# A DeltaNet stage with its steps turned: first blocks substituted on VectorE, level products on small tiles, seven weight halves subtracted on GpSimd

## The reference

```
qkv = silu(causal_conv(proj[..., :GD_QKV], conv_w))      # 4 taps
G = cumsum(g) within a chunk
gamma = exp(where(incl, G[..., :, None] - G[..., None, :], -inf))
a_mat = where(strict, kk * gamma * beta, 0)
t_mat = triangular_solve(a_mat + eye, eye)               # inverse of a unit lower triangle
u = t_mat @ (v * beta);  w = t_mat @ (k * beta * exp(G))
step: v_new = u - w S;  o = q_g S + qk v_new;  S = decay S + k_g^T v_new
out = (rmsnorm(o) * gain * silu(z)) @ w_out
```

## Time and profile before

| | us |
|---|---|
| median of 3 runs | 2547.61 (2543.11 to 2550.33) |
| the profiled execution | 2547.9 |
| its span | 2545.8 |
| TensorE busy | 2377.2 (93%) |
| VectorE busy | 1282.2 (50%) |
| ScalarE busy | 960.3 (38%) |
| GpSimd busy | 486.9 (19%) |
| chain that ended last: TensorE's share | 83% |
| transfers: mean rate | 80 GB/s |

### The profile page before, as it was taken

How to read it: one execution, slowest core, us unless ns; L and a number is a source line. 1 busy time by engine, 2 the same in 40 slices (tenths; PEclk the granted TensorE clock), 3 DMA queues, 4 the chain that set the end, 5 groups by cost and what they waited for, 6 DMA issues and landing times.

```text
span 2545.8 us, 30868 instructions
## 1 busy us (share of the span) xinstructions
PE 2377.2 (93%) x10878; PEld 1942.2 (76%) x10878; DVE 1282.2 (50%) x1548; ACT 960.3 (38%) x1313; POOL 486.9 (19%) x384
## 2 busy tenths in 40 slices
PE   8999998998999999999999975989898889999997
PEld 7888876787788888788888754777777667888886
DVE  5544337665364443554443685455555442644533
ACT  5233335554443233333233454333333343423332
POOL 2222001100221110111111235343121101211100
PEclk9999999998999999999999996899899999999999
DMA  5332332221223323233333220111111213223232
GB/s 166 95 94 77 101 107 63 69 72 66 66 84 98 99 82 96 86 99 99 99 82 94 73 85 10 40 50 51 50 50 52 73 50 98 72 94 99 85 97 66
DMA packets 67561, 203.11 MB, mean 80 GB/s; under 512 B 8320, under 2 KB 12544, under 8 KB 67488
## 3 DMA queue, kind: packets, MB, share of 16 engines
q1 hardware_dynamic: 67488, 202.13, 25.5%
HBM read 199.94 MB, written 2.16 MB: 79 GB/s over the span
## 4 chain that ended last, share of the span: by engine, by line
PE 83%; DVE 6%; ACT 4%; issue 4%; POOL 2%; DMA 0%; DVEq 0%; SPq 0%; ACTq 0%; POOLq 0%
PE bank L1413 70%; PE bank L1595 6%; ACT w_hi L503 1%; DVE gate L1048 1%; POOL gd_o L1348 1%; POOL sq L1345 1%; PE bank L1680 1%; DVE up L1048 1%; DVE pre L1042 1%; PE bank L1693 1%; PE bank L1722 1%; PE bank L1560 0%; DVE w_lo L845 0%; PE bank L1714 0%; PE bank L1686 0%
## 5 line engine op out<-in xcount | busy, mean ns | idle before, releaser
L845 DVE TENSOR_TENSOR w_lo<-raw,w_hi 128x1024 fp32r<-128x1024 f32 x405 | 586.2, 1465 | 563.1 <-ACT w_hi L503 563.0
L1413 PE MATMUL bank<-h_hi,w_hi 128*128 128x512 f32 x1760 | 702.8, 399 | 44.3 <-DVE h_lo L849 31.3
L1413 PE MATMUL bank<-h_hi,w_lo 128*128 128x512 f32 x1760 | 692.4, 393 | 0.0
L1413 PE MATMUL bank<-h_lo,w_hi 128*128 128x512 f32 x1696 | 666.4, 393 | 0.0
L503 ACT ACTIVATE w_hi<-raw 128x1024 fp32r<-128x1024 f32 x405 | 426.4, 1055 | 538.1 <-PE bank L1413 533.3
L1413 PEld LDWEIGHTS bank<-h_hi,w_hi 128*128 128x128 f32 x1760 | 335.3, 191 | 123.5 <-issue 40.3
L1413 PEld LDWEIGHTS bank<-h_hi,w_lo 128*128 128x128 f32 x1760 | 334.6, 190 | 71.5
L1413 PEld LDWEIGHTS bank<-h_lo,w_hi 128*128 128x128 f32 x1696 | 323.0, 190 | 69.5 <-issue 3.1
L1287 POOL TENSOR_TENSOR y<-y,up 128x512 f32<-128x512 f32 x88 | 173.9, 1976 | 744.6 <-DVE up L888 671.2
L1413 PE MATMUL bank<-act_hi,w_hi 128*128 128x512 f32 x704 | 277.4, 394 | 0.0
L1413 PE MATMUL bank<-act_hi,w_lo 128*128 128x512 f32 x704 | 276.0, 392 | 0.0
(11 more groups left out here) (254 smaller groups left out, 2467.6 us busy)
## 6 DMA issues: line engine op xcount, KB each, us to landing
raw<-in_ffn_in SPq DMA_DIRECT2D x172, 512.0 KB, 3.5
raw<-in_gd_in SPq DMA_DIRECT2D x49, 512.0 KB, 5.5
raw<-in_ffn_out SPq DMA_DIRECT2D x64, 384.0 KB, 3.1
raw<-in_ffn_out SPq DMA_DIRECT2D x64, 320.0 KB, 2.9
raw<-in_hg_in SPq DMA_DIRECT2D x32, 512.0 KB, 3.5
raw<-in_gd_out SPq DMA_DIRECT2D x16, 512.0 KB, 3.7
raw<-in_hg_out SPq DMA_DIRECT2D x8, 512.0 KB, 3.4
g_bc<-g_rows SPq DMA_DIRECT2D x8, 512.0 KB, 4.3
```

What stands on the lines that cost most here:

```text
L845: nc.vector.tensor_tensor(w_lo[:, r, :], raw[:, r, :], w_hi[:, r, :].bitcast(f32), ALU.subtract).then_inc(lo_split, 1)
L1413: ins = nc.tensor.matmul(dst, w, moving[ml][:, k, :], start=first and n == 0 and (wl, ml) == (0, 0), stop=last and n == len(ks) - 1 and wl ...
```

## The change

**Turned steps.** `step(j)` now runs the recurrence of group j - 1 first and then the levels of group j; group 0's levels come before step 1, and `last_step` has only the recurrence of group 7. TensorE's step is written with named pieces; `each` is 2 in step 1 and 1 else. Step 1 has seven units (10 to 16), steps 2 to 7 five, the last two. Units 5 to 7 change places (query first). The sums and products of keys 4 to 7 move into step 1.

```diff
+                    new_values(g, 0)
+                    piece(each)
+                    state_add(g, 0)
+                    piece(each)
+                    attend(g, 0)
+                    for t in (1, 2):
+                        state_read(g, t)
+                        piece(each)
+                        new_values(g, t)
+                        piece(each)
+                        state_add(g, t)
+                        piece(each)
+                        attend(g, t)
+                    state_read(g, 3)
+                    piece(each)
+                    new_values(g, 3)
+                    if level:
+                        key_gram(j)
+                        key_transpose(j)
+                    piece(each)
+                    attend(g, 3)
+                    piece(2 * each)
+                    out_sums(g)
+                    if level:
+                        piece(4)
...
+                            late_key_sum(5)
+                        piece()
+                        level_p5(j)
+                        piece(2)
...
+                        level_t5(j)
+                        scores(j)
+                        piece()
+                        value_transpose(j, 0)
+                        piece(2)
+                        level_u5(j)
+                        piece(2)
...
+                            late_key_product(5)
+                        piece(2)
+                        level_p6(j)
+                        piece(2)
```

```diff
+                def to_lanes_first():
+                    dve.wait_ge(kkd_made, 4)
+                    for b in range(4):
+                        rows = slice(b * SUB, (b + 1) * SUB)
+                        src = four_banks[rows, :].rearrange("p (n q) -> p q n", q=P)[:, rows, :]
+                        nc.vector.transpose(lane_t[rows, :, :], src.unsqueeze(2).to_broadcast([SUB, SUB, 2, 4 * NT])).then_inc(lane_kk, 1)
+                    lanes_done(0)
+
+                def to_lanes_second():
+                    dve.wait_ge(kkd_copied, 4)
+                    dve.wait_ge(diag_ready, 2)
+                    nc.vector.transpose(lane_t, kk_diag.unsqueeze(2).to_broadcast([P, SUB, 2, 4 * NT])).then_inc(lane_kk, 1)
+                    lanes_done(1)
+
+                def substitute(cols):
+
+                    for c in cols:
+                        rows = SUB - 1 - c
+                        part = lane_tmp[:, 0:rows * c].rearrange("p (i k) -> p i k", k=c)
+                        below = lane_t[:, c + 1:SUB, 0:c]
+                        if c == 1:
+                            dve.wait_ge(lane_ready, 2)
+                        wait(dve, lane_sub, 2 * (c - 1))
+                        TT(part, lane_t[:, c + 1:SUB, c:c + 1].to_broadcast([P, rows, c]),
+                           lane_t[:, c:c + 1, 0:c].to_broadcast([P, rows, c]), ALU.mult).then_inc(lane_sub, 1)
+                        dve.wait_ge(lane_sub, 2 * (c - 1) + 1)
+                        TT(below, below, part, ALU.add).then_inc(lane_sub, 1)
 
```

```diff
+                def lo(n):
+                    u = first_unit[s] + n
+                    pool.wait_ge(lo_split, u + SKEW)
+                    pool.wait_ge(hi_split, u + 1 + SKEW)
+                    TTp(w_lo[:, u % RING, :], raw[:, u % RING, :], w_hi[:, u % RING, :].bitcast(f32), ALU.subtract).then_inc(lo_split, 1)
+                lo(6)
+                lo(7)
                 pool.wait_ge(lanes_loaded, 16 * 8)
                 TTp(lane_w[:], lane_g[:, 0, :, :], lane_g[:, 1, :, :], ALU.subtract).then_inc(lane_w_ready, 1)
```

```diff
+                def level_p5(n):
+                    pe.wait_ge(at_ready, 2 * (n + 1))
+                    pe.wait_ge(base_ready, n + 1)
+                    pe.wait_ge(q_logged, 1)
+                    for n_t in range(TILES):
+                        cols = slice(n_t * SUB, (n_t + 1) * SUB)
+                        MM(bank[3][32:64, cols], at[0:32, n_t, 32:64], half_6[0:32, n_t, 0:SUB], start=True, stop=True)
+                        ins = MM(bank[3][96:128, cols], at[64:96, n_t, 96:128], half_6[64:96, n_t, 0:SUB], start=True, stop=True)
+                    ins.then_inc(p5_made, 1)
+
+                def level_t5(n):
+                    pe.wait_ge(p5_ready, n + 1)
+                    pe.wait_ge(kt_ready, n + 1)
+                    for n_t in range(TILES):
+                        ins = MM(bank[4][32:64, n_t * SUB:(n_t + 1) * SUB], inv_t[32:64, n_t, 32:64], prod5[32:64, n_t, :], start=True, stop=True)
+                    ins.then_inc(t5_made, 1)
+
+                def level_u5(n):
+                    pe.wait_ge(vt_ready, 2 * n + 1)
+                    for n_t in range(TILES):
+                        cols = slice(n_t * SUB, (n_t + 1) * SUB)
+                        MM(bank[5][0:32, cols], prod5[32:64, n_t, :], inv_t[32:64, n_t, 32:64], start=True, stop=True)
+                        ins = MM(bank[5][64:96, cols], prod5[96:128, n_t, :], inv_t[96:128, n_t, 96:128], start=True, stop=True)
+                    ins.then_inc(u5_made, 1)
+
+                def level_p6(n):
+                    pe.wait_ge(t5_ready, n + 1)
+                    if n:
+                        pe.wait_ge(vt_ready, 2 * n + 2)
+                    for n_t in range(TILES):
+                        ins = MM(bank[6 if n else 2][CH:P, n_t * CH:(n_t + 1) * CH], at[0:CH, n_t, CH:P], half_6[0:CH, n_t, :], start=True, stop=True)
+                    ins.then_inc(p6_made, 1)
+
+                def level_u6(n):
+                    pe.wait_ge(p6_ready, n + 1)
+                    pe.wait_ge(u5_ready, n + 1)
+                    for n_t in range(TILES):
+                        ins = MM(bank[3][0:CH, n_t * CH:(n_t + 1) * CH], half_6[CH:P, n_t, :], inv_t[CH:P, n_t, CH:P], start=True, stop=True)
+                    ins.then_inc(u6_made, 1)
+
+                def new_values(g, t):
```

**VectorE's step**, for g > 0 (the taps stand in brackets):

```diff
+                    else:
                         gate_out(g - 1, 1)
+                        memory(g, 0)
+                        if j == 4:
...
+                        residual(g, 1)
+                        if j == 2:
+                            to_lanes_second()
+                        out_gate(g - 1, 1)
+                        value_decay(g, 1)
+                        memory(g, 1)
+                        residual(g, 2)
+                        value_decay(g, 2)
+                        query_drain(j)
+                        memory(g, 2)
+                        query(j, (0,))
+                    residual(g, 3)
+                    query(j, (1,))
+                    lo(n0 + 4)
+                    query(j, (2, 3))
+                    log_gamma(j, 0)
+                    log_gamma(j, 1)
+                    value_drain(j, 0)
+                    value(j, 0, (0, 1, 2))
+                    out_norm(g)
+                    decayed_keys(j)
+                    if g == 0:
+                        key_norm(4)
+                        key_norm(5)
...
+                    value(j, 0, (3,))
+                    lo(n0 + 5)
+                    query_norm(j)
+                    value_drain(j, 1)
+                    value(j, 1, (0,))
+                    lo(n0 + 6)
+                    probs_out(j)
+                    if g == 0:
+                        key_norm(6)
+                        key_norm(7)
+                    value(j, 1, (1, 2, 3))
+                    gate_out(g, 0)
+                    lo(n0 + 7)
+                    out_gate(g, 0)
```

More of the change, by code:

```diff
@@ L708, in out_root, with out_square @@
+                def out_square(g):
+                    for e in range(2):
+                        act.wait_ge(og_made, 2 * g + e + 1)
+                        wait(act, og_ready, 2 * (g - 1) + e + 1)
+                        nc.scalar.activation(y[:, e, :], bank[(7, 2)[e]][:], ACT.Square).then_inc(og_squared, 1)
                 def out_root(g):
@@ new lines, in log_gamma, with decayed_keys @@
+                def log_gamma(n, e):
+                    dve.wait_ge(g_loaded, 16 * (n + 1))
+                    wait(dve, og_made, 2 * n)
+                    h = head_row(n, e)
+                    for t in range(NT):
+                        ins = TS(attn[:, e * NT + t, :], g_bc[:, e, t * P:(t + 1) * P], tab[:, 5, t, h:h + 1], 0.0, ALU.add, ALU.min)
+                    ins.then_inc(d_made, 1)
+                def decayed_keys(n):
+                    if n:
+                        dve.wait_ge(kk_made, n)
+                    for e in range(2):
+                        dve.wait_ge(gam_ready, 2 * n + e + 1)
+                        TT(at[:, tiles(e), :], attn[:, tiles(e), :], by_tile(3 if n else 2, P), ALU.mult).then_inc(at_ready, 1)
@@ new lines, in query_norm, with probs_out, value_decay @@
+                def query_norm(n):
+                    dve.wait_ge(q_root, n + 1)
+                    STT(out=qn, in0=q_a, scalar=float(P) ** -0.5, in1=qn, op0=ALU.mult, op1=ALU.mult).then_inc(qn_ready, 1)
+                def probs_out(n):
+                    dve.wait_ge(qk_made, n + 1)
+                    for e in range(2):
```

(52 more changed lines are left out.)

879 lines of the change are left out of this document (477 added, 402 removed).

## The result

The changed kernel takes 2426.14 us (2423.61 to 2426.75 over four runs), against 2545.58 for the kernel before in the same series: a ratio of 0.9527, interval 0.951 to 0.9544. The forecast was 2462, with a range of 2428 to 2512. The direction was right, the gain was 40 per cent larger than forecast, and the time lies 2 us under the range. It is the first rival, "everything fits" at 2432, that came about. The profiled execution took 2426.58, with a span of 2424.7.

The account below looks back on a forecast made before the run. TensorE was taken as the bound, losing time to waits and half clock. Head to 1557, then 73, 323 and 28 us gave 1981 against 2066.7: 85.7 less than 2547.9, so 2462.2, range 2428 to 2512.

Parts of the forecast that it names:

- the first rival: Whole stage: no waits in the steps and small tile records at half of 0.062 us, giving 2432 us; chance 0.15.
- The head: Stretch up to the first product with an inverse: VectorE substitutes instead of GpSimd, so that product starts at 1557, before 1608.35.
- Step 1: First turned step, with twelve more sixths of a unit, four key sums and products, and 4 us of waits: 73 us.
- Steps 2 to 7: Six turned steps at 53 us each, against 61.27 before, plus 5 for extra block passes: 323 us.
- The two terms from the earlier trace: Each step of 61.27 us would lose its 5.5 us of TensorE waits and 4.9 us of half-clock loss.
- I take zero, and keep -3.5 and +2.7: Level products in 32x32 and 64x64 tiles: no net gain per group counted, with -3.5 to +2.7 us kept as bounds.
- About 1 us there and 1 at the query's sum: Remaining waits in a step, behind GpSimd's spreading and at the query's sum: 2.1 us, raising 50.9 to 53.
- lower bound: Shortest time allowed for a step, 50.9 us: 61.27 without its waits and clock loss, level tiles counted at zero.
- The second pass: Second pass of blocks through VectorE in steps 2 and 4: 5 us added.
- The last part: From the first product of group 7 to the output projection: 28 us, against 27.75 before.
- The second, a GpSimd that holds VectorE: GpSimd's spreading delays VectorE and so TensorE: steps of 57 us, head 10 later, total 2496; chance 0.22.
- The third: Rival for the level products: 32x32 tile records do not overlap, 0.22 to 0.27 us apart, 134 more, total 2596; chance 0.04.

## Why the prediction was right in kind and short in size

- **The head: right in the sum, by errors against each other.** 1557 forecast, 1559.65 measured (in a trace that stands 0.6 later from the start). The blocks were in the lanes at 1513.4, not 1504.3. The last normalisation ended at 1499.45, not 1497: I counted 2.5 us for two low halves pushing VectorE, and the taps and normalisations lost 6.7 (6.84 - 2.33 and 3.43 - 1.29). The larger error lies between there and the lanes. I had one key product of 0.9 us, and TensorE had three to do, because after the first it waited 3.6 us for a table of factors from ScalarE (`tab`, an output of ScalarE, not its table load):

```profile
1496.13 1.16 PE L1847 MATMUL bank<-gd_o 128*128 128x128 f32 x8 [2.95 <-DVE gd_o L1172]
1500.86 4.92 PE L1847 MATMUL bank<-gd_o 128*128 128x128 f32 x24 [3.56 <-ACT tab L903]
```

  So the transposes began at 1505.82 where 1497.9 was forecast, and with the product and the diagonal they took 7.6, not 6.4. The 60 operations took 21.9, not 26.3: their formula (21.4) held, and the 4.9 for GpSimd were nothing, since the low halves of units 10 and 11 ended at 1504.3 and 1512.2, before the first of the 60. From there to TensorE's restart it was 5.1, not 7.0, since the restart hung on VectorE's drain and not on the whole spreading. The levels took 19.1, as the 19.7 said.
- **Step 1:** 69.7 against 73, 3.3 less. The small tiles' 3.4 would account for it; that it is they and not the 4 us of waits in that term was not tried for this step.
- **Steps 2 to 7: the step that failed.** I had 53 each; a clean one takes 46.96. The two terms from the earlier trace rows hold: 5.5 of waits became 0.6, and the clock's 4.9 came back. "I take zero, and keep -3.5 and +2.7" was wrong: the tiles are worth -3.44 (large tiles in the changed kernel). "About 1 us there and 1 at the query's sum" was wrong too: 0.6 at the query's sum and nothing at GpSimd's spreading. Six times 6.04 are 36.2, and the forecast missed by 36.1; the other parts nearly cancel, with 2.7 more in the head, 3.3 less in step 1 and 1.4 more in the second pass. Waits 4.9, clock 4.9 and tiles 3.4 make 13.2 of the 14.3 gained a step; 1.1 I can't place.
- **The "lower bound" of 50.9 was none.** It left the tiles at zero, though the low end for them stood three lines further down. With it the bound is 47.4, and the measured step lies 0.4 below.
- **The second pass:** 4.6 us in step 2 and 1.9 in step 4, 6.4 together, for a term of 5.
- **The last part:** 1945.65 - 1917.81 = 27.8, for 28.
- **Rivals.** The first, at 0.15, happened, and the time lies another 6 us below it. The second, a GpSimd that holds VectorE, is a real thing in the head, where it cost VectorE 6.7 us, and costs nothing that shows in a step: step 3, with GpSimd busy for 25.3 us, took 47.01, and 1.3 us more on VectorE cost nothing either. The third is refuted by the records of a 32x32 product, TensorE's timeline:

```profile
1852.16 0.21 PE L1922 MATMUL bank<-half,at 32*32 32x32 f32 x1
1852.17 0.21 PE L1923 MATMUL bank<-half,at 32*32 32x32 f32 x1
...
1852.78 0.50 PE L1824 MATMUL bank<-h_hi,w_lo 128*128 128x512 f32 x1
```

The two tiles start 0.01 us apart, and 32 records start within 0.50 us: 0.016 each, 0.031 for each of the pairs. The product t5, with 16 records in one tile, holds TensorE just as long, 0.61 us (1854.81 to 1855.42), as these 32 in two tiles do. The rule of the Trainium skill (TensorEngine Tiling, Key Properties) that different tiles run in parallel is borne out by it. What a change of tile size costs is small: the next unit matmul starts 0.62 us after the first record, 0.12 after the last. I had set it at 0.1 to 0.2.

I worked out both the tiles' value at half spacing and the full removal of waits, gave each to the rival, and let the forecast stand at the cautious end of both at once.

## What to carry to other kernels

Once an order leaves TensorE neither waiting nor at half clock, each microsecond of its own work is worth a microsecond: behind the first group the same tiles were worth 1.8 us a group in the old order and 3.44 in the new one, and in all 17.6 us against about 30. Take the row's scaling for such a term rather than zero, and let the low end of a range hold all favourable terms together. Work moved to GpSimd beside a busy VectorE is not free; look for a stretch in which VectorE waits. And when a head is shortened, see first whose drain frees the bank that the next step wants.

## What the runs showed of the hardware that was not expected

**GpSimd and VectorE stretch each other, VectorE up to threefold.** The same 60 operations keep GpSimd busy for 42.3 us beside a VectorE that works for 36.3 of 49.0 us, and for 29.9 beside a waiting one. Three of VectorE's taps take 6.84 us beside GpSimd and 2.33 alone. VectorE's drain out of PSUM was not stretched: 0.68 us at 1539.70, beside GpSimd's spreading, as elsewhere.

**The clock's return after a long wait differs between executions of one program.** The low halves on VectorE were profiled twice. Both traces have the wait of 24.1 us. Windows of the first, from the end of its wait, then of the second (columns as in the windows above; the third number from the end is the clock):

```profile
1535.96:1541.00 5.04, 5.04 (x44) 3.68 (x44) 4.93 (x6) 0.63 (x1) 2.25 (x2) 0.71 0.00 0
1541.00:1545.50 4.50, 3.80 (x77) 3.45 (x76) 4.36 (x5) 2.47 (x7) 2.68 (x2) 1.00 0.02 4
```

```profile
1536.67:1541.60 4.93, 4.93 (x41) 3.63 (x42) 4.83 (x6) 0.53 (x1) 2.24 (x2) 0.50 0.00 0
1541.60:1546.00 4.40, 4.40 (x28) 3.49 (x29) 4.26 (x6) 1.73 (x5) 2.68 (x2) 0.50 0.00 0
1546.00:1550.00 4.00, 4.00 (x55) 3.59 (x54) 3.86 (x6) 0.84 (x3) 1.42 (x2) 0.50 0.01 4
```

In the first, TensorE is back at 2.4 GHz 2.7 us after it restarts. In the second it stays at 1.2 GHz up to 1554 us, 17 us after its restart, and was busy without a pause all that time. The first product with an inverse comes 15.2 us after the restart in one and 21.7 in the other, and the executions took 2418.6 and 2426.33 us. The changed kernel's three traces all have 19.0 to 19.3 there. Over the ten timed executions of this variant the mean granted clock falls into two groups: 0.976 or 0.977 in four, which took 2416.2 to 2418.6 us, and 0.972 in six, which took 2423.1 to 2426.3. So a difference of up to 7 us between two versions of this head can't be told from a single execution of each. The variant's spread goes with the clock's return. Why the clock returned early in some executions is open, and so is whether the place of the low halves has a part in it.
